# A hybrid attention and state-space layer: C's convolution off the matmul engine, deferred products, earlier exponentials, a second bank

## The reference

```python
proj = x @ w_in                                   # q, k, v, gates, z_ssd, xbc, dt
att  = fox_attention(q, k, v, log_f) * silu(z_att)
xbc  = silu(causal_depthwise_conv(xbc, conv_w, conv_b))     # 4 taps, 4096 channels
xs, Bm, Cm = split(xbc)                           # 2048 | 8 groups x 128 | 8 groups x 128
# per group (4 heads of 64), chunks of 128 tokens:
decay = exp(where(causal, seg, -inf))
cb    = einsum('bclgn,bcsgn->bcgls', Cc, Bc)
y_diag = einsum(cb * decay, Xdt)                  # within the chunk
states = einsum(Bc, decay_end, Xdt)               # what the chunk adds to the state
carry  = carry * chunk_decay + states             # a scan over the chunks
y_off  = einsum(Cc, carry_before, exp(a_cs))
y = (y_diag + y_off + d_skip * xs) * silu(z_ssd)
y = rmsnorm per group(y) * ssd_norm_w
out = layer_norm(alpha * x + concat(att, y) @ w_out)
```

## Time and profile before

| | us |
|---|---|
| median of 3 runs | 1933.17 (1931.16 to 1936.24) |
| the profiled execution, its own time | 1933.39 |
| its span on the slowest core (core 3) | 1931.8 |
| spans of the 8 cores | 1916.5 to 1931.8 |

### The profile page before, as it was taken

One profiled execution on the slowest core, in us unless ns is written; L12 is line 12 of the kernel. 1 busy time (PEld: TensorE's weight loads), 2 busy tenths in 40 slices (PEclk: granted clock), 3 DMA queues, 4 the chain that ended last, 5 costly groups with the idle time before them and its releaser, 6 DMA issues.

```text
span 1931.8 us, 35062 instructions; the slowest of 8 cores (1916.5 to 1931.8 us)
## 1 busy us (share of the span) xinstructions
PE 1829.2 (95%) x11798; PEld 1020.0 (53%) x11798; DVE 984.2 (51%) x2177; ACT 721.9 (37%) x1786; POOL 547.8 (28%) x730
## 2 busy tenths in 40 slices
PE   5997999999999888999999999999999997999997
PEld 2444445445445554665666656666566653444443
DVE  0032322322222344767767676767676666565565
ACT  1122443443344564555555555555555540000000
POOL 3000000000000004655656565655656550000000
PEclk9998999999999998999999999999999998999999
DMA  9908241642811521543636353633565566434431
GB/s 145 144 6 122 40 83 39 96 72 52 117 21 39 99 47 50 105 103 77 132 75 129 78 115 84 114 91 85 126 163 121 137 173 209 163 131 151 138 131 55
DMA packets 165121, 196.05 MB, mean 101 GB/s; under 512 B 96776, under 2 KB 123560, under 8 KB 158128
## 3 DMA queue, kind: packets, MB, share of 16 engines
q1 hardware_dynamic: 145552, 125.62, 24.4%
q0 software_dynamic: 19392, 68.20, 22.0%
HBM read 215.27 MB, written 42.22 MB: 133 GB/s over the span
## 4 chain that ended last, share of the span: by engine, by line
PE 81%; DMA 7%; DVE 5%; issue 3%; ACT 2%; POOL 1%; SPq 0%; DVEq 0%; ACTq 0%; POOLq 0%
PE bank L338 81%; DMA vz_slab<-wpack 2%; DMA w_out_bf<-wob 2%; DMA attst<-atg 2%; DMA ysm_r<-yn_r 1%; ACT P L350 1%; ACT tt L350 1%; DVE MT_r L354 1%; DVE t_r L354 0%; DVE xt L364 0%; SPq L111 0%; ACT vp L369 0%; DVE nrw_r L364 0%; DVE rstd_r L360 0%; DVE atg L364 0%
## 5 line engine op out<-in xcount | busy, mean ns | idle before, releaser
L338 PE MATMUL bank<-xT_bf,slab 128*128 128x512 bf16 x2048 | 480.0, 381 | 21.1 <-DMA xT_bf<-xT 21.1
L338 PEld LDWEIGHTS bank<-xT_bf,slab 128*128 128x128 bf16 x2048 | 197.5, 98 | 238.9 <-issue 27.3
L338 PE MATMUL bank<-vz_slab,xT_bf 128*128 128x512 bf16 x1024 | 250.5, 389 | 17.3 <-DMA vz_slab<-wpack 10.6
L338 PE MATMUL bank<-w_out_bf,mb 128*128 128x512 bf16 x1024 | 233.7, 381 | 0.0
L338 PE MATMUL bank<-xT_bf,slab_r 128*128 128x512 bf16 x1024 | 231.5, 379 | 0.0
L350 ACT ACTIVATE dec_r<-abc_r,nb_tok 128x128 bf16<-128x128 f32 x512 | 205.2, 401 | 36.3 <-ACT dec_r L350 1.1
L354 POOL TENSOR_TENSOR t_r<-t_r,xd_r 128x256 f32<-128x256 f32 x120 | 99.7, 831 | 334.6 <-DVE t_r L354 328.0
L350 ACT ACTIVATE tt<-bank 128x512 f32<-128x512 f32 (+1 forms) x256 | 138.7, 542 | 138.4 <-PE bank L338 128.5
L338 PEld LDWEIGHTS bank<-vz_slab,xT_bf 128*128 128x128 bf16 x1024 | 99.5, 100 | 126.8 <-issue 28.3
L338 PEld LDWEIGHTS bank<-w_out_bf,mb 128*128 128x128 bf16 x1024 | 100.6, 98 | 121.6 <-issue 2.5
L338 PEld LDWEIGHTS bank<-xT_bf,slab_r 128*128 128x128 bf16 x1024 | 98.9, 98 | 113.6
(11 more groups left out here) (136 smaller groups left out, 2521.0 us busy)
## 6 DMA issues: line engine op xcount, KB each, us to landing
abc_r<-acs_d SPq DMA_DIRECT2D x128, 256.0 KB, 3.5
slab<-wpack POOLq DMA_DIRECT2D x20, 1024.0 KB, 9.9
xt<-x_tok SPq DMA_DIRECT2D x16, 1024.0 KB, 6.0
out<-xt SPq DMA_DIRECT2D x64, 256.0 KB, 2.3
wob<-w_out POOLq DMA_DIRECT2D x24, 512.0 KB, 25.2
slab_r<-wpack POOLq DMA_DIRECT2D x12, 1024.0 KB, 9.7
mb<-mixs SPq DMA_DIRECT2D x16, 768.0 KB, 5.5
xT_bf<-xT POOLq DMA_DIRECT2D x16, 512.0 KB, 45.3
```

The costliest lines, as they stand in the source:

```text
L338: return p.op("pe", lambda e: e.matmul(outap, lhsT, rhs, start=start, stop=stop), reads, writes, signal)
```

## The change

Six things are done together.

- The convolution of C leaves PE. ACT forms bias plus the first tap from `uT` into a new f32 tile `cv`, three DVE instructions add the other taps, and ACT's tanh and DVE's product now read `cv`. The diagonal matrices of C go from the DMA and the memory. The order of the blocks becomes 3, 2, 0, 1.
- `SILU_L` puts off each product: it is issued one filling step after its tanh (all open ones at a tile's mark and end). The transpose of B is put off by two steps.
- The exponentials of chunk n+2 are issued in chunk n (`front_exp`), with three buffers; loads and masks of `abc` go one chunk ahead with them.
- The products of alternate chunks use banks 1 and 4 instead of bank 1 alone; `xd` has one buffer for two.
- The generator runs ahead of the chunks by a cost of 3.5 (`LEAD`), so that block 3 of the next tile is projected in the last chunk of this one; the tile's cost is set to 25.7 for 26.8.
- Three kinds of DVE instruction (the copy of 3 columns of `uT`, the carry's multiply, the first step of the norm) become `scalar_tensor_tensor` instructions of the same result.

```diff
@@ conv weights and bias of C as columns; C's diagonal blocks dropped from convdg (2048 -> 1536)
+    cbc = np.zeros((128, 8, 5), np.float32)
+    for g in range(8):
+        ch = 3072 + g * 128 + np.arange(128)
+        cbc[:, g, 0:4] = conv_w[:, ch].T
+        cbc[:, g, 4] = conv_b[ch]
...
-        dec_bf = [RA.alloc([128, 512], BF16, "dec%d" % i) for i in range(2)]
+        dec_bf = [RA.alloc([128, 512], BF16, "dec%d" % i) for i in range(3)]
-        xd = [RA.alloc([128, 256], F32, "xd%d" % i) for i in range(2)]
+        xd = [RA.alloc([128, 256], F32, "xd0")] * 2
...
+        defq = []
+        def later(k, fn):
+            defq.append([k + 1, fn])
+        def tick(flush=False):
+            ready = []
+            for it in list(defq):
+                it[0] -= 1
+                if flush or it[0] <= 0:
+                    defq.remove(it)
+                    ready.append(it[1])
+            for fn in ready:
+                fn()
+            if flush and defq:
+                tick(True)
+        def SILU_L(outap, psum_ap, reads, writes, in_view=None, tt_view=None):
+            k = tti[0] % 2
+            tti[0] += 1
+            ACT(ttb[k][:, :], psum_ap, AF.Tanh, reads, [b_tt[k]], scale=0.5)
+            tv = ttb[k][:, :] if tt_view is None else tt_view(ttb[k][:, :])
+            pv = psum_ap if in_view is None else in_view(psum_ap)
+            later(1, lambda: STT("dve", outap, tv, 1.0, pv, ALU.add, ALU.mult, [b_tt[k]] + list(reads), writes))
...
-                CPY("dve", uT[:, :, 0:3], uT[:, :, 512:515], [], b_uT)
+                STT("dve", uT[:, :, 0:3], uT[:, :, 512:515], 1.0, uT[:, :, 512:515], ALU.mult, ALU.max, [], b_uT)
...
+            def conv_C():
+                c0 = g * 5
+                ACT(cv[:, :], uT[:, 3, 0:512], AF.Identity, [b_uT[3], b_cwb], [b_cv], bias=cwb[:, c0 + 4:c0 + 5],
+                    scale=cwb[:, c0:c0 + 1])
+                def taps():
+                    for k in range(1, 4):
+                        STT("dve", cv[:, :], uT[:, 3, k:k + 512], cwb[:, c0 + k:c0 + k + 1], cv[:, :], ALU.mult,
+                            ALU.add, [b_uT[3], b_cwb], [b_cv])
+                later(1, taps)
+                later(3, lambda: SILU_L(CT[par][:, :], cv[:, :], [b_cv], [b_CT[par]]))
...
-            yield from proj(2)
             yield from proj(3)
+            for i_, v in enumerate(proj(2)):
+                if i_ == 0:
+                    conv_C()
+                yield v
...
+            yield from proj(0)
             yield from conv_fm(2)
-            yield from proj(0)
-            yield from conv_fm(3)
             yield from proj(1)
...
             yield from conv_tok(0)
-            tr_B()
+            later(2, tr_B)
             yield from conv_tok(1)
...
+        def front_exp(n):
+            g, c = n // 16, n % 16
+            if n < 128:
+                for hl in range(4):
+                    ACT(dec_bf[n % 3][:, hl * 128:(hl + 1) * 128], abc[n % 4][:, hl * 128:(hl + 1) * 128], AF.Exp,
+                        [b_abc[n % 4], b_ssdc], [b_dec[n % 3]], bias=nb_tok[:, c, 4 * g + hl:4 * g + hl + 1])
...
         def back_pe(n):
+            yb = 1 + 3 * i2
-                MM(banks[1][:, hl * 64:(hl + 1) * 64], MT_bf[i2][:, hl * 128:(hl + 1) * 128],
+                MM(banks[yb][:, hl * 64:(hl + 1) * 64], MT_bf[i2][:, hl * 128:(hl + 1) * 128],
...
-                TT("dve", v4(carry[:, :]), v4(carry[:, :]), bc4(cd_bc[:, c, hs4]), ALU.mult, [b_ssdc], [b_carry])
+                STT("dve", v4(carry[:, :]), v4(carry[:, :]), 1.0, bc4(cd_bc[:, c, hs4]), ALU.mult, ALU.mult, [b_ssdc],
+                    [b_carry])
...
-            TS("dve", x, x, 4.0 * EPS, None, ALU.add, None, [], bs)
+            STT("dve", x, x, 4.0 * EPS, x, ALU.add, ALU.max, [], bs)
...
-        A_COST = 26.8
+        A_COST = 25.7
+        LEAD = 3.5
...
-            base = state["spent"] if n > 124 else A_COST * cq / 4
+            base = state["spent"] if n > 124 else A_COST * cq / 4 + LEAD
+            def fill(part):
+                upto = base + A_COST * part
+                if n < 124 and upto > A_COST:
+                    run_to(Q + 2, upto - A_COST)
+                else:
+                    run_A(upto)
...
                     front(n + 1)
-                load_abc(n + 4)
-                mask_abc(n + 2)
+                front_exp(n + 2)
+                load_abc(n + 5)
+                mask_abc(n + 3)
                 back_ew(n)
...
-            run_A(base + A_COST / 8)
+            fill(0.125)
...
-            run_A(base + A_COST / 4)
+            fill(0.25)
```

More of the change, by code:

```diff
@@ L297, in make_convdg @@
         wg = conv_w[:, group_channels(g)].reshape(4, 4, 128)
-        for j in range(4):
+        for j in range(3):
             for k in range(4):
                 dgs[g, r, j, k, r] = wg[k, j]
-    return dgs.reshape(8, 128, 2048)
+    return dgs.reshape(8, 128, 1536)
 def build_program(dbg=False, phases=3):
@@ L1038, in post_st, with start_gen, run_to @@
             b_mix[c].append(bm)
-        state = {"gen": None, "spent": 0.0, "mark": True}
+        state = {"gen": None, "spent": 0.0, "mark": True, "q": 0}
+        def start_gen(k):
+            state.update(gen=gen_A(k) if k < 32 else gen_out(), spent=0.0, mark=k >= 32, q=k)
+        def run_to(k, upto):
+            while state["q"] < k:
+                run_A(1e9)
+                start_gen(state["q"] + 1)
+            run_A(upto)
         def run_A(upto, need_mark=False):
```

75 lines of the change are left out of this document (40 added, 35 removed).

## The result

The changed kernel is slower. The median of its four executions is 2042.33 us; against the kernel before, run beside it (1932.16), the ratio is 1.056, with a 95% interval of 1.053 to 1.059. That is the direction I forecast, and more than I forecast: 1985 was the prediction and 2016 the top of its range. The profiled execution took 2037.67, its span on core 3 is 2036.1, so against the profiled execution of before there are 104.3 us to explain.

A forecast was written before the change was run, and what follows sets the result against it. PE was taken as the bound, with 81% of the chain. Matmuls removed (-1.085), today's loss (-0.20) and waits (+0.8, +2.1) gave +1.6 us a tile, 49 over 30.75 tiles, plus 2 at the end: 1985, range 1927 to 2016.

The forecast's parts named there:

- What bounds the kernel: SSD stage: PE bounds, losing only 0.20 us a tile; at the second chunk's end DVE and POOL have no margin left.
- Second and third head: Second chunk: evacuation and norm delay MT and Xdd; PE waits 1.4 us for MT, 2.1 in all (1.6 to 2.4).
- the sum: Per tile -1.085, -0.20, +0.8 and +2.1 give +1.6 us; times 30.75 is 49, plus 2 at the end: 1985.
- First head: First chunk: three taps on DVE wait for cv and collide with POOL; PE waits 0.2 to 1.5 us, 0.8 taken.
- Third and fourth chunk: Third and fourth chunk of a tile: DVE has no norm and no taps there, so nothing is added.
- the end of the stage: Chunk 127: loads queued earlier on SP ahead of the transposes lengthen PE's wait for MT by 0 to 4 us, 2 taken.
- More than my bounds: Rival: collisions also catch the carry's multiply and push the next chunk's Xdd; over 2017 us, chance 0.07.
- Taps free of POOL: Rival: first chunk's taps don't collide with POOL, waits 0.2 and 2.1, +1.0 us a tile, 1966; chance 0.20.
- PE stays the bound: Rival: DVE's burst behind the second head is absorbed, all 1.285 us a tile come back, 1894; chance 0.14.
- even: Rival: the waits sum to between 1.1 and 1.5 us a tile, time within 0.3%; chance 0.05.
- Edits at nothing: Early exponentials, two banks, deferred products, one xd buffer and smaller diagonal loads were counted as gaining nothing.
- What I had said would show it: Signs: heads at 28.6 us a tile, PE's waits 50 to 80 for MT, 20 to 30 for Xdd, cv rows over 0.75.

The follow-up runs named there:

- e2: Changed kernel with the norm's 12 instructions, and the yn that needs them, issued behind the second chunk's MT; 1999.39 us, ratio 1.035 to the kernel before.
- e1: Changed kernel with 11 matmuls of unread results in PE's pauses for MT and Xdd in each third chunk; 2012.18 us, ratio 1.043 to the kernel before.
- e11: Kernel before, C's convolution still on PE, with each third chunk's MT and Xdd products computed four times so that PE pauses; 2021.89 us, ratio 1.047.
- e10: Changed kernel with the three kinds of DVE instruction put back from scalar_tensor_tensor to what they were; ratio 1.056 to the kernel before.
- e9: Changed kernel with norm behind MT, uT evacuated by ACT, two Newton steps for three, early POOL mask, lead 4.3; 1916.92 us, ratio 0.992 to the kernel before.
- e12: Kernel before with the repeated MT and Xdd products of e11, and matmuls of unread results filling the two pauses; 2001.42 us, ratio 1.037.
- e4: Changed kernel with the first chunk's exponentials issued behind cv on ACT; 2032.56 us, ratio 1.052 to the kernel before.

## Why the prediction was right, and where it failed

**What bounds the kernel, right.** PE had no margin at the third head, and the 33 us of matmuls taken off it came back as waits. The matmuls did go (160 instructions), and no engine became the bound by its share: DVE is busy for 52%. It is late at two places.

**Second and third head, right in the mechanism, just over the bounds.** The second chunk takes 7.33, where 7.46 followed from 6.06 and a wait of 1.4. The third takes 7.90 without a fall of the clock. PE's own work there is the rest of the tile, 25.67 less 7.30, 6.05 and 5.59 = 6.73, so its wait costs 1.17. Together 1.28 + 1.17 = 2.45 a tile, against 2.1 taken and 2.4 as the most. e2 shows that the norm, with the `yn` behind it, is what does it. The chain came as worked out: `Xdd`'s matmul starts 8.61 behind the second head, for 8.7. What was off is where PE would want it: the sum had 0.28 behind its head, but without a wait it follows by 0.12, as at the head at 1093.22 of the earlier trace rows (kernel before):

```profile
1093.34 0.27 PE L338 MATMUL bank<-Xdd_r,B_tok_r 128*128 128x256 bf16 x1
```

8.61 less 6.05 and 0.12 is 2.44, the measured 2.45.

**First head, right in its mechanism, at the upper bound.** 8.80 less 7.30 is 1.5, the bound with every collision; in the first tile of a group (7 of 30 first chunks between the heads) it is 7.77 less 7.19, 0.58; in the mean 1.23. The taps begin 4.0 behind the head, for the 3.8 that followed from a `cv` of 0.59; it took 0.81. I took 0.8 for the wait, "near the middle", because I couldn't tell whether the mask gets in ahead of the third tap. It does: it starts at 1134.25, when the taps are less than half done. The middle between two bounds was no estimate. POOL's timeline of the kernel before doesn't answer the question either. There the mask starts 6.6 us behind the first head (at 1085.90), just as the third tap was to end (6.5); in the changed kernel it starts 5.6 behind it. From the timelines of DVE and POOL in the kernel before:

```profile
1086.93 0.69 DVE L364 SCALAR_TENSOR_TENSOR gz_tok_r<-tt,bank 128x512 bf16<-128x512 f32 x1 [1.30 <-ACT cb_bf_r L350]
...
1088.92 0.42 DVE L354 TENSOR_TENSOR t_r<-t_r,bank 128x256 f32<-128x256 f32 x1
...
1092.48 1.15 POOL L354 TENSOR_TENSOR abc_r<-abc_r,mask 128x512 f32<-128x512 f32 x1
```

The product of z's gate (`gz_tok`), which stood in front of `back_ew` there, is done before the head now. So the second `t`, for which POOL waits, starts 1.8 behind the head (1130.48) in the place of 3.0, and POOL's instructions, the mask among them, come earlier. Deferred products and the generator's lead can both do this; no run separates them, and the prediction had put the first of them at nothing.

**The step that failed.** "Third and fourth chunk: [...] nothing is added." Something is: after the pauses PE runs at half its clock for some 3.3 us in 19 of 31 third chunks, 1.65 us each, 31 us, 1.02 a tile. The sum had every wait cost its own length and no more. e1 takes this loss away without shortening another chunk, and e11 makes it without the change. It is the one term that lifts the time beyond the range: with waits at the bounds alone the prediction had 2017, and e1, where the chunks are as long as in the changed kernel but for the clock, has 2012.

The terms against the sum: (1.23 - 0.8) + (2.45 - 2.1) + 1.02 = 1.80 a tile, times 30.75 is 55; the end of the stage took 0.6 for the 2 assumed, so 54. The profiled execution lies 2037.67 - 1985 = 52.7 above the forecast.

There was a hint. The earlier trace rows hold a head behind a pause of 10.4 us, and its four matmuls take 0.37 where every head of the earlier trace rows takes 0.28; the granted clock is 0.50 there. That row was quoted for its wait, and its duration was not read. The Trainium skill (TensorE: Matmul & The Clock Gate, section "HAM oscillation — how this bites in real kernels") describes bursts of matmuls that start at the lower clock because PE waits for DMA between them, in waits longer than these. I didn't weigh it, since the waits in question were near 1 us; the traces show the lower clock behind such short waits too, in some tiles and not in all. So that a pause can cost the clock was to be read beforehand; that pauses of 1 us do it was not.

**The rivals.** "More than my bounds", at 0.07, is the side on which it came out, but its mechanism, collisions that catch the carry's multiply and push `Xdd` of the next chunk, was not what took the time there. It occurs in small: behind the third head the carry's multiply takes 0.89 for 0.42, and `Xdd` beside it 0.79 for 0.61, yet the two waits together are only 0.05 over the 2.4. "Taps free of POOL" falls by the 3.75, "PE stays the bound" and "even" by PE's 97.8 us of waits. "Edits at nothing" was tested for the three kinds of instruction alone (e10), and holds there, though two of the three (the copy and the norm's first step) had one SBUF input before, and not two as the prediction says. PE waits for none of the others by name, but one of them may have brought the mask forward, as said above.

**What I had said would show it.** Waits for `MT` of 50 to 80 (67.6, and 78 with the stage's start) and `cv` rows well over 0.75 (1.04) came true, `Xdd` of 20 to 30 (30.2) at its edge, and the heads at 28.6 a tile didn't (30.28). The text named the end of the stage as what I'd have missed if the tile was right; it named nothing for a chunk that takes longer without a wait.

## What to carry to other kernels

A pause of the matmul engine isn't priced by its length alone: where two pauses of about 1 us follow each other, look at the granted clock behind them, and add what the next matmuls lose. Moving work off the engine that bounds the kernel pays only if the engines that feed it are ahead at every place where it comes for their results; so read their margin at each such place, and not their busy share, and give the freed time back in the queue's order (the norm behind `MT`, evacuations on the idler engine) before expecting a gain. An edit that shortens one wait may be given back at the next one: compare the chunks one by one.

## What the runs showed of the hardware

- Two pauses of 1.1 and 1.0 us on PE, four small matmuls apart, brought the granted clock from 1.00 to 0.50 for about 3.3 us in 19 of 31 tiles (changed kernel), and pauses of 1.3 and 1.0 in 15 of 31 (e11). In e2, with other pauses at the third and fourth head (1.7 to 2.1 us for `MT` and 0.19 for `Xdd` in front of the low fourth chunks), it fell in 8 chunks; in e9, with single waits of up to 1.1 us, in none. Eleven matmuls of about 0.16 us in the two pauses kept it at 1.00 in the third chunk of every tile (e1, e12).
- A mask on POOL and three taps on DVE, 1.15 and 2.70 us without each other, took 1.60 and 3.75 side by side. A DVE instruction of 0.41 took 1.34 beside the mask (e4).
